# Stage changes of a three-layer model in one launch: two more weight buffers, output blocks left in PSUM, activation table loaded earlier

## What is computed

```python
h = h + rms_norm(mixer(rms_norm(h, mix_norm_pre)), mix_norm_post)
f = swiglu(rms_norm(h, ffn_norm_pre))          # (silu(g) * u) @ w_down
h = h + rms_norm(f, ffn_norm_post)
```

## Time and profile before

| | us |
|---|---|
| median of 3 runs | 2197.82 (2196.25 to 2198.82) |
| the profiled execution's own time | 2198.08 |
| its span in the profile | 2195.9 |
| TensorE busy | 2096.7 (95%) |
| VectorE busy | 1179.0 (54%) |
| ScalarE busy | 707.8 (32%) |
| granted TensorE clock, mean | 0.983 |

### The profile page before, as it was taken

How to read it: one execution, slowest core, us unless ns; L and a number is a source line. 1 busy time by engine, 2 the same in 40 slices (tenths; PEclk the granted TensorE clock), 3 DMA queues, 4 the chain that set the end, 5 groups by cost and what they waited for, 6 DMA issues and landing times.

```text
span 2195.9 us, 25960 instructions
## 1 busy us (share of the span) xinstructions
PE 2096.7 (95%) x10181; PEld 1724.3 (79%) x10181; DVE 1179.0 (54%) x1975; ACT 707.8 (32%) x1040; POOL 9.7 (0%) x23
## 2 busy tenths in 40 slices
PE   7999999999999999999997999999998799999997
PEld 5887888888788797787876788888786577888885
DVE  5646544422775757747555844432489656444324
ACT  4224322211523323333233522221343554222212
POOL 0000000000000000000000000000000000000000
PEclk9999999999999999999988999999999899999998
DMA  4762222222124151141411222232222112222221
GB/s 166 112 109 77 96 96 96 96 96 96 60 98 131 58 148 64 58 134 58 135 39 39 77 96 96 96 104 98 96 86 77 39 61 94 96 96 96 99 101 49
DMA packets 35914, 198.53 MB, mean 90 GB/s; under 512 B 3912, under 2 KB 4457, under 8 KB 14457
## 3 DMA queue, kind: packets, MB, share of 16 engines
q1 hardware_dynamic: 28248, 182.13, 23.8%
q10 hardware_dynamic: 6656, 12.58, 2.7%
q0 software_dynamic: 928, 2.70, 2.5%
HBM read 181.14 MB, written 3.67 MB: 84 GB/s over the span
## 4 chain that ended last, share of the span: by engine, by line
PE 85%; DVE 8%; ACT 4%; issue 2%; DMA 0%; SPq 0%; DVEq 0%; ACTq 0%
PE bank L1373 78%; PE bank L1596 2%; ACT w_hi L474 2%; DVE c L1249 2%; PE bank L1558 1%; PE bank L1574 1%; DVE w_lo L804 1%; DVE w_lo L802 1%; DVE p L1100 0%; DVE work L857 0%; DVE h L862 0%; ACT p L600 0%; PE bank L1746 0%; DVE v1s L1071 0%; DVE work L878 0%
## 5 line engine op out<-in xcount | busy, mean ns | idle before, releaser
L1373 PE MATMUL bank<-x_hi,w_hi 128*128 128x512 f32 x1760 | 700.7, 398 | 19.5 <-DVE x_lo L815 15.9
L1373 PE MATMUL bank<-x_hi,w_lo 128*128 128x512 f32 x1760 | 687.7, 391 | 0.0
L1373 PE MATMUL bank<-x_lo,w_hi 128*128 128x512 f32 x1760 | 687.2, 390 | 0.0
L802 DVE TENSOR_TENSOR w_lo<-w_raw,w_hi 128x2048 fp32r<-128x2048 f32 x131 | 299.7, 2291 | 469.6 <-ACT w_hi L474 469.6
L1373 PEld LDWEIGHTS bank<-x_hi,w_hi 128*128 128x128 f32 x1760 | 331.6, 188 | 101.1 <-issue 29.7
L1373 PEld LDWEIGHTS bank<-x_hi,w_lo 128*128 128x128 f32 x1760 | 331.5, 188 | 70.8
L1373 PEld LDWEIGHTS bank<-x_lo,w_hi 128*128 128x128 f32 x1760 | 331.9, 189 | 67.1 <-issue 1.4
L474 ACT ACTIVATE w_hi<-w_raw 128x2048 fp32r<-128x2048 f32 x131 | 249.8, 1907 | 375.8 <-PE bank L1373 375.8
L1373 PE MATMUL bank<-ff_hi,w_hi 128*128 (+1 forms) x528 | 205.8, 390 | 4.1 <-DVE work L878 4.1
L1373 PE MATMUL bank<-ff_hi,w_lo 128*128 (+1 forms) x528 | 205.4, 389 | 0.0
L1373 PE MATMUL bank<-ff_lo,w_hi 128*128 (+1 forms) x528 | 205.4, 389 | 0.0
(11 more groups left out here) (189 smaller groups left out, 2055.8 us busy)
## 6 DMA issues: line engine op xcount, KB each, us to landing
w_raw<-w_all SPq DMA_DIRECT2D x167, 1024.0 KB, 4.9
qk<-qk_next ACTq DMA_DIRECT2D x32, 384.0 KB, 10.6
w_raw<-w_all SPq DMA_DIRECT2D x8, 256.0 KB, 6.4
h<-x_t SPq DMA_DIRECT2D x4, 512.0 KB, 7.2
out_t<-h SPq DMA_DIRECT2D x8, 256.0 KB, 2.0
skew<-erow POOLq DMA_DIRECT2D x8, 192.0 KB, 8.7
bias<-skew POOLq DMA_DIRECT2D x8, 128.0 KB, 3.4
pos_i<-pos SPq DMA_DIRECT2D x1, 256.0 KB
```

The source lines that it names most:

```text
L802: ins = v.tensor_tensor(w_lo[p][:, part], w_raw[p][:, part], hi, ALU.subtract)
L1373: ins = mm(out, b if flip else a, a if flip else b, start=start and n == 0, stop=stop and n == 2, **kw)
```

## The change

- `w_hi` and `w_lo` get two more buffers each, at byte 49152 of the shared region. Units LAST+1 and LAST+2 of each change use them (`slot`); all others stay at u % 2. LAST+1 and LAST+2 are rounded in `down` (or before `post_norm`), LAST+1 is split there too, LAST+2 in `post_norm`, and LAST+3 is rounded in `post_norm` after the third square.
- In changes 1, 2 and 4 the blocks are finished in the order 4, 5, 6, 7, 0, 1, 2, 3, and blocks 1, 2, 3 stay in PSUM; in change 6 blocks 1 to 7 stay. ScalarE's square and VectorE's scaling read them there. The matmuls without use write bank 4.
- The table set with Ln and Exp is loaded at the start of `down`, after sine and cosine, and after the LayerNorm's SiLU loop; the loads in `post_norm` and before the attention are gone.
- What lies in the extra buffers' space moves: `v1s` is set to one after the fourth QKV unit, `u2`'s edge is cleared after the second IN2 unit, and the eight loads of `bias2` wait for two units of IN2. In the attention FFN_B is rounded in step 27 and split in step 29, in the convolution part the first feed-forward units wait for the mixer's tiles.

```diff
+KEPT = [(), (1, 2, 3), (1, 2, 3), (), (1, 2, 3), (), (1, 2, 3, 4, 5, 6, 7)]
+Y_ORDER = [[4, 5, 6, 7, 0, 1, 2, 3] if len(kept) == 3 else list(range(KC)) for kept in KEPT]
+def slot(u):
+    if u - 1 in LAST_ROWS[1:]:
+        return 2
+    return 3 if u - 2 in LAST_ROWS[1:] else u % 2
...
+        for n in range(2):
+            w_hi.append(sb(f"w_hi{2 + n}", [P, UNIT], F32R, at=region + 49152 + 16384 * n))
+            w_lo.append(sb(f"w_lo{2 + n}", [P, UNIT], F32R, at=region + 49152 + 16384 * n + 8192))
...
+            pool.wait_ge(unit_done, IN2 + 2)
...
-                if u >= 2:
+                if u - 1 in LAST_ROWS[1:]:
+                    act.wait_ge(unit_done, u - 2)
+                elif u - 2 in LAST_ROWS[1:] or u - 3 in LAST_ROWS[1:]:
+                    act.wait_ge(unit_done, u - 3)
+                elif u >= 2:
                     act.wait_ge(unit_done, run(i, per, u - 1))
...
             def post_norm(t):
-                for m in range(KC):
-                    act.wait_ge(y_copied, KC * (t - 1) + m + 1)
...
-                    nc.scalar.activation(dst, y[:, m, :], ACT.Square).then_inc(ysq_done, 1)
-                if LAST_ROWS[t] + 2 < UNITS:
-                    round_unit(LAST_ROWS[t] + 2)
-                nc.scalar.preload_act_table_set("natural_log_exp_and_others")
+                for i, m in enumerate(Y_ORDER[t]):
+                    if m not in KEPT[t]:
+                        act.wait_ge(y_copied, copied_count(t, i))
+                    elif i < KC - 1:
+                        act.wait_ge(y_done, 7 * (t - 1) + i + 1)
+                    else:
+                        act.wait_ge(unit_done, LAST_ROWS[t] + 1)
...
+                    nc.scalar.activation(dst, bank[m][:] if m in KEPT[t] else y[:, m, :],
+                                         ACT.Square).then_inc(ysq_done, 1)
+                    if i == 2 and t < 6:
+                        round_unit(LAST_ROWS[t] + 3)
...
             def pre_norm_rstd(t):
-                round_unit(LAST_ROWS[t] + 3 if t else 2)
+                if t == 0:
+                    round_unit(2)
...
             def down(u0):
+                nc.scalar.preload_act_table_set("natural_log_exp_and_others")
                 with act.Fori(0, 4) as i:
                     for l in range(2):
                         round_unit(u0 + l + 2, i, 2)
-                for l in (8, 9):
+                for l in (8, 9, 10):
...
                 if last + 2 < UNITS:
-                    rest_unit(last + 1)
                     rest_unit(last + 2)
...
-                        mm(bank[1][:, 0:3 * P], ident_b[:], mask_b[:], start=True, stop=True)
+                        mm(bank[4][:, 0:3 * P], ident_b[:], mask_b[:], start=True, stop=True)
```

More of the change, by code:

```diff
@@ L98, with copied_count @@
 LAST_ROWS = [None, FFN_A - 1, QKV - 1, FFN_B - 1, IN2 - 1, FFN_C - 1, UNITS - 1]
+KEPT = [(), (1, 2, 3), (1, 2, 3), (), (1, 2, 3), (), (1, 2, 3, 4, 5, 6, 7)]
+Y_ORDER = [[4, 5, 6, 7, 0, 1, 2, 3] if len(kept) == 3 else list(range(KC)) for kept in KEPT]
+def copied_count(t, i):
+    return sum(KC - len(kept) for kept in KEPT[1:t]) + i + 1
+def slot(u):
+    if u - 1 in LAST_ROWS[1:]:
+        return 2
+    return 3 if u - 2 in LAST_ROWS[1:] else u % 2
 PI_CLAMP = 3.1415925
@@ L471, in round_parts @@
             def round_parts(u, parts, last):
-                p = u % 2
                 for part, g in parts:
-                    ins = nc.scalar.activation(w_hi[p][:, part], w_raw[p][:, part], ACT.Copy,
+                    ins = nc.scalar.activation(w_hi[slot(u)][:, part], w_raw[u % 2][:, part], ACT.Copy,
                                                scale=1.0 if g is None else g)
@@ L579, in _ @@
                     round_unit(l + 2)
-            for l in range(3):
+            for l in range(2):
                 round_unit(CONV_OUT + l + 2)
+            act.wait_ge(mix_ready, KC)
+            for l in range(2):
+                round_unit(FFN_A + l)
             post_norm(1)
@@ L658, in _ @@
                     mix_hi_block(2 + n // 2)
+                if n == 27:
+                    act.wait_ge(at_scores, 16 * KC)
+                    round_unit(FFN_B)
                 fill = fill_of(n)
@@ L672, in _ @@
                 mix_hi_block(b)
-            round_unit(FFN_B)
+            act.wait_ge(at_av, 16 * KC)
+            round_unit(FFN_B + 1)
             post_norm(3)
@@ L771, in _ @@
             round_unit(OUT2B + 1)
-            round_unit(FFN_C)
+            for l in range(2):
+                round_unit(FFN_C + l)
             post_norm(5)
@@ L829, in post_norm @@
                 last = LAST_ROWS[t]
-                for m in range(KC):
-                    if m < KC - 1:
-                        dve.wait_ge(y_done, 7 * (t - 1) + m + 1)
-                    else:
-                        dve.wait_ge(unit_done, last + 1)
-                    if t == 3:
+                for i, m in enumerate(Y_ORDER[t]):
+                    if m not in KEPT[t]:
+                        if i < KC - 1:
+                            dve.wait_ge(y_done, 7 * (t - 1) + i + 1)
+                        else:
+                            dve.wait_ge(unit_done, last + 1)
+                    if m in KEPT[t]:
+                        pass
+                    elif t == 3:
                         v.tensor_tensor(y[:, m, :], part[:, m, :], bank[m][:], ALU.add).then_inc(y_copied, 1)
@@ L920, in down @@
                 rest_unit(u0 + 10)
+                if u0 + 11 < UNITS:
+                    rest_unit(u0 + 11)
             dve.wait_ge(par_loaded, 16)
@@ L1019, in _ @@
                     rest_unit(l + 2)
-            for l in range(2):
+            for l in range(3):
                 rest_unit(CONV_OUT + l + 2)
@@ L1035, in _ @@
             v.memset(cm, 0.0).then_inc(at_out, 1)
-            for b in range(3):
-                order.mark(v.memset(v1s[b][:, :, :, HD:2 * HD], 1.0))
-            order.wait()
             dve.wait_ge(rcol_ready, 1)
@@ L1162, in _ @@
                 elif lam == 6:
+                    order.wait()
                     take_v0()
+                if lam == 3:
+                    for b in range(3):
+                        order.mark(v.memset(v1s[b][:, :, :, HD:2 * HD], 1.0))
                 if 1 <= lam <= GROUP - 3:
@@ L1200, in _ @@
                     attend(3, pair, name)
+                if n == 29:
+                    rest_unit(FFN_B)
                 if n < 2:
```

39 lines of the change are left out of this document (21 added, 18 removed).

## The result

The changed kernel took 2183.01 us (median of 4 runs, 2180.93 to 2183.89) beside 2197.03 (4 runs, 2195.78 to 2198.82): 14.0 us less, ratio 0.9935, 95% interval 0.9920 to 0.9951. The profiled execution was the fastest of the four: 2180.93, span 2179.1, so 16.8 us shorter than the profile of before. Of those, 11.5 will turn out to be the stage changes' own. The 5.1 others lie between the changes: 3.4 of them go with TensorE's granted clock alone, and 1.7 with the clock and the moved clearing of v1s together. (0.1 is from the start up to change 1.)

The account below looks back on a forecast made before the run. TensorE, busy 95% of the span, was taken as the bound, with gains only at the six stage changes. Terms of 2.3, 2.8, 0.8 and 0.7, 2.9 and 1.25 sum to 10.75 us: median 2187.1, range 2183.5 to 2191.5.

Parts of the forecast that it names:

- parts 1, 2, 4: Stage changes: earlier rounding and splitting, third unit between squares, table load moved; 1.89 and 1.28 us leave the path to Ln.
- a sign of being wrong: Before a stage change's first square: ScalarE seen waiting for a load there would show the prediction wrong.
- Changes 1 and 4: First and fourth stage change: gap to the next stage's first product falls 2.3 us, in the first from 9.06 to 6.8.
- TensorE is free at E+6.8: E ends the old stage's last product; 30 fillers at 0.1625 us (4.88) end at E+6.8, the last thing awaited.
- Change 2: Second stage change: sum of squares at E+1.3 as before, next first product at 574.95 instead of 577.75, 2.8 us gained.
- Change 6: Last stage change, no product behind it: everything from the statistics moves with them, 1.25 us gained.
- Changes 3 and 5: Third and fifth stage change: VectorE cannot catch up, 0.2 us lost; TensorE free at E+8.3, gains 0.7 and 0.8 us.
- The convolution behind change 4: Stage after the fourth change, paced by VectorE: second unit ends earlier, so sigmoid, rounding and all taps start 2.9 us sooner.
- the first rival: Kept blocks cost VectorE's scaling 0.06 us more each to read from PSUM; 1.0 us comes back, 2188.1; chance 0.12.
- Part 3: Blocks left in PSUM: copy (0.69) leaves the last block's path; first statistics product at E+0.1 instead of E+1.39.
- the second rival: Half is lost: adds fall behind, or TensorE's clock falls differently after the fourth change; 2190.5 to 2193; chance 0.15.
- part 5: Moved memsets, DMAs and attention splits: clearing v1s uses idle VectorE time; FFN_B's split loses 0.1 us, bounds 0 and 1.2.

Follow-up runs that it names:

- the experiment: The changed kernel with FFN_B's rounding and split put back behind the attention steps: median 2185.08 us, ratio 0.9943.

## Why the prediction was right in kind and too small in size

- **What goes in front of Ln** (parts 1, 2, 4): right in all six changes. ScalarE is seen waiting for a load in front of its squares, which the prediction had named as a sign of being wrong, but in front of the rounding of LAST+2, where the prediction itself had it land (183.1 in change 1; 183.24 measured), and no first square came late by it. Of the two things that left, the table load was worth nothing once the rounding had gone, and alone 0.8 us; the prediction counted both in one sum and did not need to part them. That VectorE's two splits stood beside ScalarE's chain, 0.16 us shorter, it did not say.
- **Changes 1 and 4**, 2.3 forecast, 2.41 measured: "TensorE is free at E+6.8" was 6.65. The next first product comes 4.74 behind the first filler, not 4.88.
- **Change 2**, 2.8: 2.75. **Change 6**, 1.25: 1.33.
- **Changes 3 and 5**, 0.8 and 0.7: 1.09 and 1.10. Wrong step: VectorE "cannot catch up: I count 0.2 us lost". It can, and the statistics product came at E+1.38 as before. (The sum also has 0.8 for 9.03 less 8.3, which is 0.73.) In change 3 its adds ran 0.31 late behind the rounding and were level again three blocks on, at 1.20 us for an add and a block where TensorE gives 1.36:

```profile
1199.96 0.69 DVE L888 TENSOR_TENSOR work<-work 128x512 f32<-128x512 f32 x1 [0.31 <-ACT work L525]
...
1201.17 0.69 DVE L888 TENSOR_TENSOR work<-work 128x512 f32<-128x512 f32 x1
1202.37 0.68 DVE L888 TENSOR_TENSOR work<-work 128x512 f32<-128x512 f32 x1
1203.65 0.68 DVE L888 TENSOR_TENSOR work<-work 128x512 f32<-128x512 f32 x1
```

- **The convolution behind change 4**, 2.9: its first taps' input comes 40.90 behind E before (1624.87) and 38.12 after (1611.25), 2.8. Right. And FFN_B's earlier split did not cost 0.1 but saved 0.33, by the experiment.
- **PSUM as a source**: nothing, as forecast. The groups by form, after:

```profile
L897 DVE SCALAR_TENSOR_TENSOR work<-y,par_s,work 128x512 f32<-128x512 f32 x32 | 23.9, 745 | 8.8 <-ACT work L511 8.8
L897 DVE SCALAR_TENSOR_TENSOR work<-bank,par_s,work 128x512 f32<-128x512 f32 x16 | 11.9, 744 | 0.0
L525 ACT ACTIVATE work<-y 128x512 f32<-128x512 f32 x32 | 19.6, 627 | 31.0 <-DVE y L878 19.1 <-DVE y L876 7.1 <-DVE y L880 2.8
L525 ACT ACTIVATE work<-bank 128x512 f32<-128x512 f32 x16 | 9.6, 599 | 8.1 <-PE bank L1420 5.2 <-DVE work L888 2.8
```

  745 beside 744 ns: nothing, and the first rival falls. Part 3's estimate from the Trainium skill ("VectorE: DVE Perf Modes", The TRN2 errata) had 65 ns more for a PSUM source; this trace doesn't agree.
- **The sum**: with these terms 11.5 (the gaps' 11.1 and 0.4 more for the taps) instead of 10.75; 0.75 of the 3.3 that were missing.
- **The failed step** is the one behind the sum: it took everything between the changes as of fixed length. It let the clock enter only as a loss, in the second rival, in one stage, and part 5 put the moved clearing of v1s at nothing, as work that "moves into idle VectorE time"; it didn't ask what the clearing had held up in its old place. What lies between the changes gave 5.1 us in the profile (4.4 in C2-C3, 0.7 in C4-C5), 2.0 in the second profile of the same program, and about 2.5 in the medians (14.0 less 11.5).
- **What the runs show in its place.** 1.7 us of C2-C3 come where both the clearing left VectorE's queue and the clock stayed at 1.00; with either one alone it is 0.4 or nothing. They are in both profiles of the changed kernel. The other 2.7 of the first profile come with a higher clock in the attention, and in the second profile the rest of C2-C3 gives nothing. The 0.7 of C4-C5 go with the clock too. Across all fourteen profiles C2-C3 lies between 630.4 and 635.6, shortest where the clock 24 to 38 us behind change 2 is 1.00 and that from 528 us to E is 0.90, longest at 0.87 and 0.86; the feed-forward stages, whose clock is 1.00 throughout in every profile, stay within 0.3. Mean granted clock: before, 0.983 to 0.986, mostly 0.984, in 45 runs; changed, 0.985 to 0.987 in nine. How much of the 2.5 in the medians is the v1s move and how much the clock stays open, and so does why the kernels that leave fewer and shorter holes at the changes get more clock: the holes are part of it at most, since kernels with the same gap behind change 2 had 0.87 and 1.00 there.
- **The range** of 2183.5 to 2191.5 was too narrow below. The window with 0.84 in the earlier trace rows was the hint. The nine runs of the one changed program spread over 4.6 us, so by an estimate from them some 2 us in either direction belong to the range of a kernel like this, whatever is changed.

## What to carry to other kernels

In front of a wait several chains often end together. Before pricing the removal of one, write down when each of the others ends: here load and rounding on ScalarE, two splits on VectorE, the fillers on TensorE lay within 1.1 us, so the table load alone gave 0.25 us at a change, the weights alone 1.1, and all together 2.4. The same holds for work that is only moved: taking the clearing of v1s out of VectorE's queue gave 0.4 us where the clock was low and 1.7 where it was full. Queue work that a stage needs early behind a step that waits anyway, in pieces near the slack of one block (0.7 us here; pieces of 0.9 behind four squares were caught up by the last one); a queue with 0.16 us of slack in each block does catch up, only slowly. And ask of a forecast of half a percent how long the stretches are in which TensorE falls to the lower clock, since their length changes from run to run and with any shift in time.

## What the runs showed of the hardware

- Two runs of one program differ by 3.0 us in one stage, with the granted clock at 0.90 and 0.87 there, and by at most 0.5 anywhere else. 2.3 of the 3.0 go with the clock; 0.7 are a longer wait for a transfer (0.98 and 0.29 us). At the lower level three-part products are 0.43 apart, at the upper 0.23.
- ScalarE squares a block from PSUM in 599 ns and from SBUF in 627 to 631; VectorE scales in 744 and 745.
- A table load takes 1.28 us, and an activation that has its input starts 0.02 us behind its end (198.88 + 1.28, Ln at 200.18).
- Ten fillers of 128x384 in bf16 take 1.62 us; twenty in place of thirty left the mean clock where it was.
